# Reordering the blocked scan of a hybrid encoder layer: levels interleaved, POOL held for the last first inverse, one side product moved

## What is computed

```
def step(S, inp):                      # per head, 64x64 state, both directions
    r_t, w_t, k_t, v_t, a_t, b_t = inp
    sa = einsum('zdhij,zdhj->zdhi', S, a_t)
    S = S * w_t[..., None, :] + sa[..., :, None] * b_t[..., None, :] + v_t[..., :, None] * k_t[..., None, :]
    y = einsum('zdhij,zdhj->zdhi', S, r_t)
    return S, y
...
kk = (k * k_k); kk = kk * rsqrt(sum(kk * kk) + 1e-12)                   # per head
y = (y - mean) * rsqrt(var + GN_EPS) * ln_w + ln_b                      # per head
out = (y + bonus) * g
```

## Time and profile before

| | us |
|---|---|
| median of 3 runs (2981.99 to 2985.01) | 2984.55 |
| the profiled execution, its own time | 2985.67 |
| its span, first to last instruction | 2983.9 |
| the scan's 20 steps, first `turn` to last `outputs` | 761.4 |
| PE busy in the span | 2688.7 (90%) |
| DVE, ACT, POOL busy | 1261.1, 659.0, 828.6 |

### The profile page before, as it was taken

How to read it: one execution, slowest core, us unless ns; L and a number is a source line. 1 busy time by engine, 2 the same in 40 slices (tenths; PEclk the granted TensorE clock), 3 DMA queues, 4 the chain that set the end, 5 groups by cost and what they waited for, 6 DMA issues and landing times. The chain is left out here.

```text
span 2983.9 us, 68051 instructions
## 1 busy us (share of the span) xinstructions
PE 2688.7 (90%) x29216; PEld 2238.9 (75%) x29216; DVE 1261.1 (42%) x2236; ACT 659.0 (22%) x1544; POOL 828.6 (28%) x644
## 2 busy tenths in 40 slices
PE   3988997997997999999999979496999999999997
PEld 2876456886886888888888845385888888888886
DVE  5003563541112444444444422465554554554545
ACT  3102550110002443333333311032101101101102
POOL 1222113322332222222322200344323323323324
PEclk6998998998998999999999989798999999999999
DMA  4111102102211000000000034342111101101113
GB/s 120 37 46 33 31 17 85 35 21 76 87 73 48 3 4 3 3 4 3 3 3 3 4 126 159 116 126 99 36 35 42 37 33 42 42 28 42 42 42 127
DMA packets 60191, 143.10 MB, mean 48 GB/s; under 512 B 12112, under 2 KB 31184, under 8 KB 59472
## 3 DMA queue, kind: packets, MB, share of 16 engines
q1 hardware_dynamic: 46176, 114.36, 11.7%
q10 hardware_dynamic: 10256, 12.49, 1.3%
q0 software_dynamic: 3552, 13.11, 1.1%
HBM read 108.48 MB, written 31.46 MB: 47 GB/s over the span
## 5 line engine op out<-in xcount | busy, mean ns | idle before, releaser
L1846 DVE TENSOR_TENSOR f<-f,ff_pd 128x512 f32<-128x512 f32 x320 | 214.4, 685 | 153.2 <-PE ff_pd L94 153.2
L1832 DVE TENSOR_TENSOR ff_sq<-ff_rl 128x512 f32<-128x512 f32 (+1 forms) x96 | 102.2, 1064 | 296.9 <-ACT ff_rl L1793 296.9
L1793 ACT ACTIVATE ff_rl<-ff_pu 128x512 f32<-128x512 f32 (+1 forms) x96 | 50.6, 527 | 760.0 <-PE ff_pu L94 760.0
L573 PE MATMUL sc_ps<-sc_xy,sc_q 64*64 64x64 f32 x3200 | 186.1, 225 | 0.0
L570 PE MATMUL sc_ps<-sc_q,sc_xy 64*64 64x64 f32 x2560 | 166.1, 228 | 5.1 <-DVE sc_q L996 4.9
L573 PEld LDWEIGHTS sc_ps<-sc_xy,sc_q 64*64 64x64 f32 x3200 | 156.1, 141 | 0.1
L850 ACT ACTIVATE sc_xy<-sc_ps 128x256 f32<-128x256 f32 x320 | 119.1, 383 | 164.3 <-PE sc_ps L573 151.1
L94 PE MATMUL ff_pu<-h2h,ff_wu0h 128*128 128x512 f32 (+1 forms) x384 | 137.1, 357 | 14.3 <-POOL ff_wu0l L1741 14.3
L996 DVE TENSOR_TENSOR sc_q<-sc_ps,sc_cs 128x128 f32<-128x128 f32 x400 | 97.4, 288 | 110.5 <-PE sc_ps L561 107.0
L570 PEld LDWEIGHTS sc_ps<-sc_q,sc_xy 64*64 64x64 f32 x2560 | 136.2, 143 | 8.2 <-DVE sc_q L996 6.5
L94 PE MATMUL ff_pu<-h2l,ff_wu0h 128*128 128x512 f32 (+1 forms) x384 | 136.8, 356 | 0.0
(11 more groups left out here) (275 smaller groups left out, 7302.2 us busy)
## 6 DMA issues: line engine op xcount, KB each, us to landing
ff_wr<-in_w_up SPq DMA_DIRECT2D x32, 512.0 KB, 3.2
ff_wr<-in_w_down SPq DMA_DIRECT2D x32, 512.0 KB, 3.2
g_dram<-gp_g ACTq DMA_DIRECT2D x16, 640.0 KB, 2.9
mb_gate<-g_dram SPq DMA_DIRECT2D x8, 1280.0 KB, 8.9
gp_w<-in_w_in SPq DMA_DIRECT2D x16, 512.0 KB, 3.5
sp_w<-in_w_in SPq DMA_DIRECT2D x15, 512.0 KB, 3.5
n_x<-in_x SPq DMA_DIRECT2D x10, 512.0 KB, 3.6
m_dram<-mb_mo POOLq DMA_DIRECT2D x8, 640.0 KB, 8.4
```

Of the source, the lines that this page charges most:

```text
L573: last = nc.tensor.matmul(y_out[g][rows, u, :], Q1[g][rows, u, :], XY[g][rows, 1, u, :], start=True, stop=True)
L1793: nc.scalar.activation(rl[u % 2][:, 0:tn], pu[b][:, 0:tn], ACT.Relu).then_inc(relu, 1)
L1832: nc.vector.tensor_tensor(sq[u % 2][:, 0:tn], rl[u % 2][:, 0:tn], rl[u % 2][:, 0:tn], ALU.mult).then_inc(squared, 1)
L1846: nc.vector.tensor_tensor(at, at, pd[d % 4][:, :], ALU.add).then_inc(added, 1)
```

## The change

- PE's levels are interleaved: chunks 0 and 1 run their `level_xy` in the same pass, chunks 2 and 3 theirs in the next pass, between the `level_q` of the next level.
- POOL's `prepare` waits for the first inverses of all four chunks of the running step before its first instruction.
- Side piece 1 moves from the levels to the state part, chunk 0, between `solved` and `state_out` (PE: `side_late`; DVE: before the state update). Pieces 0 and 2 stay at levels 0 and 2 (bonus: 2 and 4). `side_clear` is split: piece 0 and 2 before `gram_products` of g = 1, piece 1 before `by_token` of g = 1. So the count order of the pieces is 0, 2, 1.
- ACT's exponentials move from level 0 to the last chunk of the step before (and those of step 1 ahead of the loop), the tanh of the second kind both to chunk 2, and the squares of y to levels 2 and 4 and to chunk 1.

```diff
@@ POOL, prepare(q)
                 pool.wait_ge(icl_ready, q + 1)
+                if q:
+                    pool.wait_ge(y1_ready, q * GR)
                 nc.gpsimd.tensor_scalar(fac[:, :, :], icl[:, :, :], col(ct, K_A), k1a[:, ct:ct + 1],
@@ PE, side_late: new (side keeps p = 0 at l == 0 and p = 2 at l == 2, bonus at 2 and 4)
+            def side_late(ct, i):
+                c, n = ct - 1, (ct * NB + i + 1) * GR
+                pe.wait_ge(tok_ready, n)
                 if i == 0 and ct > 0:
+                    full(TOK_BANK, mean, y[c % 2], 1, mean_ps)
                 if i == 1 and ct + 1 < CT:
                     pe.wait_ge(nrm_ready, ct + 2)
+                if i == 1 and ct > 0:
+                    full(TOK_BANK, rk_ones[:, c, :], kds[c % 2], 1, bonus_ps)
...
@@ PE, the step
                 for l in range(LEVELS):
-                    for g in range(GR):
-                        level_q(q, l, g)
-                    for g in range(GR):
-                        level_xy(q, l, g)
+                    level_q(q, l, 0)
+                    if l:
+                        level_xy(q, l - 1, 2)
+                    level_q(q, l, 1)
+                    if l:
+                        level_xy(q, l - 1, 3)
+                    level_q(q, l, 2)
+                    level_xy(q, l, 0)
+                    level_q(q, l, 3)
+                    level_xy(q, l, 1)
                     side(ct, i, l)
-                side_clear(ct, i)
+                level_xy(q, LEVELS - 1, 2)
+                level_xy(q, LEVELS - 1, 3)
                 for g in range(GR):
                     state_in(q, g)
+                    if g == 1:
+                        side_clear(ct, i, 2)
                     if more and g:
                         gram_products(q + 1, g - 1)
                     if ahead and g == 0:
                         lora_products(q + 2, 0)
                     solved(q, g)
+                    if g == 0:
+                        side_late(ct, i)
+                    if g == 1:
+                        side_clear(ct, i, 3)
                     if more and g:
                         by_token(q + 1, g - 1)
@@ ACT
             for u in range(2):
                 lora_tanh(1, 1, u)
+            decays(1, 0)
+            decays(1, 1)
             for q in range(STEPS):
...
-                        if more and l == 0 and g % 2 == 1:
-                            decays(q + 1, g // 2)
                         if i == 0 and 1 <= l <= NG and g == 1 and ct + 1 < CT:
                             k_square(ct + 1, l - 1)
-                        if i == 0 and l >= 2 and g == 3 and ct > 0:
+                        if i == 0 and g == 3 and ct > 0 and l in (2, 4):
                             y_square(ct - 1, l - 2)
...
+                    if i == 0 and g == 1 and ct > 0:
+                        y_square(ct - 1, 1)
...
-                    if ahead and g >= 2:
-                        lora_tanh(q + 2, 1, g - 2)
+                    if ahead and g == 2:
+                        lora_tanh(q + 2, 1, 0)
+                        lora_tanh(q + 2, 1, 1)
+                    if ahead and g == 3:
+                        decays(q + 2, 0)
+                        decays(q + 2, 1)
```

More of the change, by code:

```diff
@@ L666, in side @@
[L666 to L679, removed]
@@ L680, in side @@
-                if i == 1 and ct + 1 < CT and l == 1:
+                p = {0: 0, 2: 2}.get(l)
+                if i == 0 and ct > 0 and p is not None:
+                    if p == 0:
+                        pe.wait_ge(y_ready, ct * NB * GR)
+                    else:
+                        pe.wait_ge(yc_ready, c * NG + 1)
+                    full(GRAM_BANK, mean, y[c % 2], p, mean_ps)
+                if i == 1 and ct > 0 and l == 0:
+                    pe.wait_ge(sqy_ready, ct * NG)
+                    by_head(GRAM_BANK, std, mean, var_ps)
@@ L681, in side @@
+                if i == 1 and ct + 1 < CT and l == 1:
+                    pe.wait_ge(tok_ready, n)
                     pe.wait_ge(sqk_ready, (ct + 2) * NG)
                     by_head(TOK_BANK, nrm, ones, ss_ps)
-                if i == 2 and ct > 0 and l < NG:
-                    if l == 0:
+                if i == 1 and ct > 0 and l == 2:
+                    pe.wait_ge(rkk_ready, ct)
+                    pe.wait_ge(std_ready, ct)
+                    full(GRAM_BANK, rk_ones[:, c, :], kds[c % 2], 0, bonus_ps)
@@ L685, in side @@
+                if i == 1 and ct > 0 and l == 4:
+                    pe.wait_ge(bv_ready, c * NG + 1)
+                    full(GRAM_BANK, rk_ones[:, c, :], kds[c % 2], 2, bonus_ps)
+                if i == 2 and ct > 0 and p is not None:
+                    if p == 0:
                         pe.wait_ge(rsb_ready, ct)
-                    if l == 2:
+                    else:
                         pe.wait_ge(yn_ready, c * NG + 1)
-                    back(bank, std, l, rsb_ps)
-                if i == 3 and ct + 1 < CT and l < NG:
-                    if l == 0:
+                    back(GRAM_BANK, std, p, rsb_ps)
@@ L691, in side @@
+                if i == 3 and ct + 1 < CT and p is not None:
+                    if p == 0:
                         pe.wait_ge(rnb_ready, ct + 2)
-                    if l == 2:
+                    else:
                         pe.wait_ge(kk_ready, (ct + 1) * NG + 1)
-                    back(bank, nrm, l, rnb_ps)
-                if i == 4 and ct > 0 and l < NG:
-                    if l == 2:
+                    back(GRAM_BANK, nrm, p, rnb_ps)
+                if i == 4 and ct > 0 and p is not None:
+                    if p == 2:
@@ L697, in side @@
                         pe.wait_ge(out_ready, c * NG + 1)
-                    full(bank, wl[:, c, 4, :], sT[:, E_GL, :], l, gate_ps)
-            def side_clear(ct, i):
+                    full(GRAM_BANK, wl[:, c, 4, :], sT[:, E_GL, :], p, gate_ps)
+            def side_late(ct, i):
+                c, n = ct - 1, (ct * NB + i + 1) * GR
+                pe.wait_ge(tok_ready, n)
                 if i == 0 and ct > 0:
-                    pe.wait_ge(yc_ready, ct * NG)
-                if i == 1 and ct > 0:
-                    pe.wait_ge(bv_ready, ct * NG)
+                    full(TOK_BANK, mean, y[c % 2], 1, mean_ps)
@@ L712, in side_clear @@
                 if i == 4 and ct > 0:
-                    pe.wait_ge(out_ready, ct * NG)
+                    full(TOK_BANK, wl[:, c, 4, :], sT[:, E_GL, :], 1, gate_ps)
+            def side_clear(ct, i, n):
+                if i == 0 and ct > 0:
+                    pe.wait_ge(yc_ready, (ct - 1) * NG + n)
+                if i == 1 and ct > 0:
+                    pe.wait_ge(bv_ready, (ct - 1) * NG + n)
+                if i == 2 and ct > 0:
+                    pe.wait_ge(yn_ready, (ct - 1) * NG + n)
+                if i == 3 and ct + 1 < CT:
+                    pe.wait_ge(kk_ready, (ct + 1) * NG + n)
+                if i == 4 and ct > 0:
+                    pe.wait_ge(out_ready, (ct - 1) * NG + n)
```

60 lines of the change are left out of this document (33 added, 27 removed).

## The result

The changed kernel takes 2931.48 us (median of four, 2928.74 to 2935.11); the kernel before took 2983.63 us beside it. The ratio is 0.9826, 95% interval 0.9809 to 0.9843: faster by 52 us, where 53 were forecast (2932, range 2919 to 2949). The profiled execution took 2935.11 us with a span of 2933.3 us. Its 20 steps, first `turn` to last `outputs`, took 709.8 us in place of 761.4: 51.6 us less, so the whole gain lies in the scan. It was the slowest of the four, 3.6 us above their median, so what follows from this one execution is good to a few us.

What follows compares the result with a forecast made beforehand. PE's waits in the scan were taken as the bound, the largest for DVE masks held by POOL. 34.4 + 9.0 + 4 + 7.5 - 1.3 = 53.6 us, taken as 53, gave 2932 us, range 2919 to 2949.

Steps and rivals of the forecast that it cites:

- stall of `turn`: At a step's start, PE's wait for DVE masks held by POOL shortens by 1.91 us in 18 steps: 34.4 us.
- clock: Lowered PE clock stretches behind five stalled step starts go, 1.5 us each: 7.5 us gained.
- side product: In chunk 0 behind `solved`, a moved side product hides PE's 0.60 us wait for ACT in 15 steps: 9.0 us.
- exponentials of step 1: Ahead of the loop, they now stand straight on PE's path: 1.3 us lost once.
- levels: Interleaving PE's levels removes delays behind side products and exponentials, less some costs: net gain 4 us.
- rival that the term is nothing: Lowered stretches come from the levels' products, not the stall, so only 46 us are gained: 2939 us; chance 0.09.
- cover of 0.60 us: Behind `solved` in the first chunk, PE's wait for ACT's copy, to be hidden by the side product.
- price of level 0: Three `level_q`, 0.70 us, cover a 0.79 us chain: 0.09 us short, times 20, 1.8 us lost.
- cover of 1.17 us: In the interleaved levels, PE products of 0.47 + 0.23 + 0.47 us hide ACT's copy with 0.05 us to spare.
- chain of 1.12 us: In the levels, from the start of `level_xy` through ACT's copy and back to PE: 0.68, 0.38 and 0.06 us.
- square roots: In steps of i = 1, the two with their table load hold PE as before, to within 0.3 us.
- rival of the late copy: The 0.05 us margin fails, each of 320 `level_q` waits 0.06 us, 19 us given back: 2951 us; chance 0.12.

Runs made afterwards that it cites:

- e1: The kernel before with only POOL's wait for the first inverses added: 2936.67 us, ratio 0.9856.
- e3: The kernel before with only the moved side product, the split `side_clear` and the squares of y at their new places: 2978.26 us, ratio 0.9990.
- e10: The changed kernel with PE's levels back in the old order: 2922.53 us, ratio 0.9804.
- e5: The changed kernel with ACT's exponentials and second tanh put back where they were: 2934.00 us, ratio 0.9842.
- e2: The kernel before with only the interleaved levels: 2980.10 us, ratio 0.9997.
- e4: The changed kernel without POOL's wait: 2974.12 us, ratio 0.9976.
- e7: The changed kernel with POOL held until the masks of level 2 in place of the first inverses: 2939.87 us, ratio 0.9859.
- e8: The changed kernel with three unread DVE mask products ahead of the last chunk's mask, a stall without POOL: 2975.47 us, ratio 0.9978.
- e11: The changed kernel again, unaltered, run beside e10 on the same chip: 2935.01 us, ratio 0.9835.

## Why the prediction was right, and where it was not

The time was right (2932 for 2931.5). POOL's wait, the clock and the side product brought time for the reasons given, the levels did not; that the sum is closer than its terms is luck. The terms, against the loop's 51.6 us:

| term | forecast | measured | from |
|---|---|---|---|
| stall of `turn` | 34.4 | 35.7 | changed against before; 35.6 in e1 |
| clock | 7.5 | 10.9 | changed against before; 11.1 in e1 |
| side product | 9.0 | 11.2 | e3; 10.3 from e1 to e10 |
| exponentials of step 1 | -1.3 | -1.2 | e5, step 0 |
| levels | +4 | -5.0 | what is left; -5.6 or -7.2 by e10, -2.7 by e2 |

**POOL's wait** held in every step. By e4, e7 and e8 it is POOL that lengthens the masks, it does so at both places where it stands beside them, and nothing else in the change touches the stall (39.0 to 39.9 us in e2, e3 and e4). The 14 traces have 2240 of these masks with two SBUF inputs. 147 are long, each beside a POOL instruction and ending 0.14 to 0.16 us behind its end; the others take 0.29 us, and none of them overlaps a POOL instruction. The Trainium skill's SBUF page (SBUF — State Buffer, section Who interferes with whom) says that a DVE instruction with two SBUF inputs contends with a POOL instruction that reads SBUF. The trace agrees, and it agrees on the other side too: L1044, with one operand in PSUM, runs beside POOL's new place and never took over 293 ns in 400 times.

POOL's work was summed wrongly by 0.2 us: 0.7, 3.9 and 5.5 are 10.1 and not 10.3. It takes 10.05 us in step 13 (1427.42 to 1437.47) and ends 11.1 us into the step, forecast 11.2; nothing hangs on it.

**The clock term** was right in kind, and too small. All five stretches at the starts went. The eight in the steps of i = 1, which I had counted as six because two of them are twice as long, became five, so about 3.4 us more came, within the 4 us that I allowed. The rival that the term is nothing is excluded by e8 and e1. In the five kernels with the stall (before, e2, e3, e4, e8) 5, 4, 8, 4 and 8 of the stalled starts are followed by a lowered stretch; in the nine without it not one start of a step is. That it was five before, and not four or eight, looks like chance: at 1.5 us each, four to eight of them would have made this term 6 to 12 us. The Trainium skill's TensorE page (TensorE: Matmul & The Clock Gate, section Why this matters for your kernels) advises only against gaps longer than these. The measurement decides: gaps of 1.9 to 2.0 us in a stream of small products did cost the clock, in 29 of 91 cases.

**The side product.** The cover of 0.60 us was read rightly, but 0.15 us of it stays (PE leaves `solved` after 0.37 us, 1444.81 to 1445.18, and not 0.23). What I put in the wrong term is the other end: a side product in the levels makes the `level_q` behind it slower by 0.18 us and the `level_xy` on both sides by 0.14 together, and one fewer of them stands there now. e10's step 13 is 0.77 us shorter than e1's, where I had 0.60: 0.45 at `solved`, 0.18 and 0.14 in the levels, by PE's starts. I had credited the 0.18 to the interleaving.

**The levels are the step that failed.** I credited 6 us to the new order for the two `level_q` behind side products, and 2 us for the exponentials, against 1.8 and 1.5 us of cost, which is 4.7 and was entered as 4. The exponentials (e5) and the price of level 0 (0.09 us a step) were right, and the squares cost little more in this order than in the old one (steps of i = 0 are 0.35 to 0.49 us longer than e10's, step 13 0.34). Two steps of the working were not right.

First, the cover of 1.17 us stood for all levels. The last level's `level_xy` has eight products and not 16, as the section on the kernel before says itself, and there the chain of 1.12 us stands against 0.93 us of cover (0.47 + 0.23 + 0.23). With the two smaller losses behind it that is 0.38 us in 20 steps, 7.6 us.

Second, the return was counted too high. I took 0.2 us behind two side products a step. One of the two is the piece that leaves the levels, and its 0.18 us go with it in either order. In the plain order of e10 0.18 us are left behind piece 0 and 0.05 behind the shorter piece 2, and the interleaved order keeps 0.05 us behind each (1431.05 - 1430.77 = 0.28 us for eight products in step 13). A step without side products shows the bare price: step 4 is 32.40 us interleaved and 31.81 in e10, 0.59 us. Step 13, with two of them, is 0.34 us longer. So the return is 0.25 us a step and not 0.4: 3.8 us in 15 steps against 11.8 in 20, a loss of 8 us by these steps, where the loop gives 5.6 to 7.2.

The square roots hold PE about as long in either order (4.9 us in the waits view before, 3.5 and one wait of 1.0 after), as forecast.

One sign of the list failed with this term: a step with side products was to take 34.3 to 34.8 us, and takes 34.68 to 35.14 (steps of i = 1 apart).

The sum came right because the misses cancel, +1.3, +3.4 and +2.2 against -9. That is luck: the levels were forecast as a gain and are a loss, and the change without them (e10) is faster than the change. The rival of the late copy (2951) was half true: not in the 320 cases that I priced, but in the 20 of the last level.

## What to carry to other kernels

Look for DVE instructions with two SBUF operands on the path, and see what POOL does beside them. A wait that orders POOL behind them cost nothing here while POOL had slack, and gave most of this gain; but a later POOL can meet the next such instruction. A stall of about 2 us in a stream of small products cost about a third more than its length here, since some were followed by a stretch at the 1.2 GHz level. Before interleaving a pipeline, compute the cover of its shortest pass and not of its usual one, and where a product moves on PE, move its copy in the other engine's queue too.

## What was not expected of the hardware

- The cost of lowered stretches doesn't follow the edits alone: e2 met 8 and e3 met 14 with the same stall as before (39.0 to 39.9 us of turn waits, 13 stretches). Between e2 and e3 this alone is 10 us of the loop, about as much as the side product's whole gain. The changed kernel itself met five in one execution and six in another (e11). Comparing "rest" and single steps at full clock separated the two; the medians did not. Why an execution meets more of them was not settled.
- The hold scales with POOL's instruction and not with DVE's: the same 128x128 mask took 0.29 us alone, 1.30 us beside a POOL instruction of 1.29 us, and 2.85 us beside one of 2.93 us, and ended 0.14 to 0.16 us behind it each time.
